# Host-side layouts, layer 0 opening on projections of raw memory, and four narrow projections per layer made wide

## The reference

```python
def hybrid_layer(x, mem, ...):
    h = rms_norm(x, norm_pre)
    proj = h @ w_in                       # 1024 x (18 blocks of 512, 8 gate columns, 5120 gates)
    y_sb = stick_breaking(sb_q, sb_k, sb_v)
    q_ml, k_ml = silu(causal_conv(ml_q, conv_q)), silu(causal_conv(ml_k, conv_k))
    h_ml = mlstm(q_ml, k_ml, ml_v, ml_i + b_igate, ml_f + b_fgate)
    y_gm = spatial_gating(gelu(gm_u), gelu(gm_v), gm_ln_g, gm_ln_b, gm_ws, gm_bs)
    y_rt = head_norm(retention(rotary(rt_q), rotary(rt_k), rt_v))
    mkv = rms_norm(mem, mem_norm) @ w_mem_kv          # 256 memory rows, 1024 -> k and v
    mem_k, mem_v = jnp.split(mkv, 2, axis=-1)
    y_xa = memory_attention(xa_q, mem_k, mem_v)
    merged = sum over 5 branches of sigmoid(gate) * (y * silu(z)) @ w_up
    return x + rms_norm(merged @ w_out, norm_post)
```

## Time and profile before

| what | us |
|---|---|
| median of 3 runs (1751.6 to 1752.3) | 1752.22 |
| span of the profiled execution | 1750.3 |
| TensorE busy in it | 1740.1 |
| VectorE busy | 1283.1 |
| ScalarE busy | 1024.5 |

### The profile page before, as it was taken

The page is one execution under the profiler, slowest core; times in us unless marked ns, Lnnn a source line. Parts: engine busy times, 40 slices in busy tenths (PEclk is TensorE's granted clock), DMA queues, the critical chain, the costliest instruction groups (busy, mean ns, idle before and its releaser), DMA issues.

```text
span 1750.3 us, 24767 instructions
## 1 busy us (share of the span) xinstructions
PE 1740.1 (99%) x9406; PEld 1512.0 (86%) x9406; DVE 1283.1 (73%) x1714; ACT 1024.5 (59%) x1417; POOL 114.3 (7%) x186
## 2 busy tenths in 40 slices
PE   9999999999999999999999999999999999999998
PEld 8988898888889888888889988888888988888887
DVE  6966676665877586757669787688778987678775
ACT  7865566454666655644555765755556656555544
POOL 5000000000000000000000000500003360000000
PEclk9999999999999999999999999999999999999999
DMA  9656654566765566565666664456665515356663
GB/s 303 193 157 178 177 169 151 175 190 186 213 181 160 166 181 175 156 181 169 191 195 197 182 192 157 144 182 193 192 186 186 171 36 181 121 169 188 188 189 109
DMA packets 204070, 306.64 MB, mean 175 GB/s; under 512 B 12362, under 2 KB 100340, under 8 KB 203824
## 3 DMA queue, kind: packets, MB, share of 16 engines
q1 hardware_dynamic: 201056, 298.91, 56.1%
q0 software_dynamic: 2896, 6.15, 1.1%
HBM read 303.97 MB, written 1.05 MB: 174 GB/s over the span
## 4 chain that ended last, share of the span: by engine, by line
PE 91%; DVE 6%; ACT 1%; issue 1%; DMA 0%; DVEq 0%; ACTq 0%
PE bank L1696 52%; PE bank L1761 22%; PE bank L1728 8%; DVE bank L1573 2%; DVE weights_lo L1056 2%; PE bank L1801 1%; PE bank L1815 1%; PE bank L2093 1%; PE bank L2111 1%; PE bank L1823 1%; PE bank L1784 1%; ACT weights_hi L583 1%; PE bank L2017 0%; PE bank L1982 0%; PE bank L2065 0%
## 5 line engine op out<-in xcount | busy, mean ns | idle before, releaser
L1056 DVE TENSOR_TENSOR weights_lo<-weights_raw,weights_hi 128x1024 fp32r<-128x1024 f32 x560 | 668.9, 1233 | 248.6 <-ACT weights_hi L583 243.7
L583 ACT ACTIVATE weights_hi<-weights_raw 128x1024 fp32r<-128x1024 f32 x560 | 574.8, 1056 | 386.0 <-DMA weights_raw<-in_w_in_dram 181.3
L1696 PE MATMUL bank<-weights_hi,h_parts 128*128 128x512 f32 x1856 | 567.6, 391 | 0.4 <-DVE h_parts L1478 0.2
L1696 PEld LDWEIGHTS bank<-weights_hi,h_parts 128*128 128x128 f32 x1856 | 348.1, 188 | 73.3 <-DVE h_parts L1478 0.6
L1696 PE MATMUL bank<-weights_lo,h_parts 128*128 128x512 f32 x928 | 348.0, 390 | 0.0
L1696 PE MATMUL bank<-weights_hi,arena_parts 128*128 128x512 f32 x928 | 270.1, 391 | 0.0
L1761 PE MATMUL bank<-h_parts,weights_hi 128*128 128x512 f32 (+1 forms) x992 | 241.0, 385 | 0.5 <-DVE arena L1110 0.4
L1696 PEld LDWEIGHTS bank<-weights_lo,h_parts 128*128 128x128 f32 x928 | 174.4, 188 | 35.3
L1696 PEld LDWEIGHTS bank<-weights_hi,arena_parts 128*128 128x128 f32 x928 | 173.6, 188 | 35.4
L1761 PEld LDWEIGHTS bank<-h_parts,weights_hi 128*128 128x128 f32 x992 | 175.3, 189 | 31.8 <-DVE arena L1110 0.9
L1696 PE MATMUL bank<-weights_lo,arena_parts 128*128 128x512 f32 x464 | 158.4, 390 | 0.0
(11 more groups left out here) (326 smaller groups left out, 1667.6 us busy)
## 6 DMA issues: line engine op xcount, KB each, us to landing
weights_raw<-in_w_in_dram SPq DMA_DIRECT2D x224, 512.0 KB, 3.7
weights_raw<-in_f_w_up_dram SPq DMA_DIRECT2D x96, 512.0 KB, 3.5
weights_raw<-in_f_w_down_dram SPq DMA_DIRECT2D x48, 512.0 KB, 3.6
weights_raw<-in_w_up_dram SPq DMA_DIRECT2D x40, 512.0 KB, 3.5
weights_raw<-in_c_w_pw_dram SPq DMA_DIRECT2D x24, 512.0 KB, 3.6
weights_raw<-in_ab_w_in_dram SPq DMA_DIRECT2D x20, 512.0 KB, 3.8
weights_raw<-in_w_mem_kv_dram SPq DMA_DIRECT2D x16, 512.0 KB, 3.6
weights_raw<-in_w_out_dram SPq DMA_DIRECT2D x16, 512.0 KB, 3.6
```

The costliest lines, as they stand in the source:

```text
L583: nc.scalar.activation(w_hi[:, q % SPLIT, 0:w], raw[:, n % RAW, 0:w], ACT.Copy).then_inc(hi_done, 1)
L1056: tt(w_lo[:, n % RAW, 0:w], raw[:, n % RAW, 0:w], w_hi[:, q % SPLIT, 0:w].bitcast(F32), ALU.subtract)\
L1696: return mm(bs[t][:, :], sp_[:, 2 * u + kk, t * P:(t + 1) * P], wp[:, kk, :], start=first and u == us[0] and kk == 0 and n == 0, stop=last ...
```

## The change

1. The host hands over the memories transposed (`memT`, `mem_2T`), all small vectors as columns (`columns`, `columns_2`) and gm_ws transposed (`gm_wsT`). The transposes on TensorE for these go, and some 50 small DMAs.
2. Layer 0 opens with mk and mv. The raw transposed memory, scaled by mem_norm's gains, is split by VectorE (L1154, L1156 of the new kernel) and projected at once; the root mean square of each memory row comes later as a factor: as a broadcast product (`mrs`, two fp32 products of 128 columns per layer) that scales mk and memT, and as ScalarE's scale on the copy of mv. The rows of the memory are still loaded, for their squares alone. x is loaded behind the first four units.
3. sb_q, ml_q, ml_k and xa_q go from `proj_F` (or its staged form) to `proj_W`. VectorE sums their banks; the convolutions read them from SBUF.

```diff
-                win(l, SBQ)
+                else:
+                    ap = kmaj("w_mem_kv", (l,))
+                    got.extend((True, ap[:, 4 * u:4 * u + 4, i * S:(i + 1) * S]) for u in range(2) for i in range(2))
+                    mem_v()
+                halved("w_in", (l,), SBQ)
...
+                if n == 4:
+                    for t, s in enumerate((x0_in, x1_in)):
+                        sp.dma_start(xs[:, t, :], A["x"][0][t * P:(t + 1) * P, :]).then_inc(s, 16)
...
+            pool.dma_start(arena[:, 6:8, :], A["mem"][0].rearrange("(t p) d -> p t d", p=P)).then_inc(mem_in, 16)
...
+            def mem_norm(src):
+
+                for t in range(NT):
+                    for n in range(2):
+                        square(src[:, t, n * 512:(n + 1) * 512], "mem", t, n)
+                for t in range(NT):
+                    act.wait_ge(vec_done, after_vec(f"mem.base{t}"))
...
+                    act.dma_start(cols[:, :], A["columns"]).then_inc(cols_in, 16)
                     log_exp_table()
+                    up_to(4)
...
+                        up_to(4 + 2 * t)
                         act.wait_ge(s, 16)
...
+                    act.wait_ge(mem_in, 16)
+                    mem_norm(rows_of(6))
+                    for t in range(NT):
+                        copy(tok(5)[:, t, :], "mv", t, ACT.Copy, f"mv{t}", scale=mem_rstd[t])
...
+                b = filled("mrs")[:, 0:S].unsqueeze(1)
                 if l == 0:
...
+                    link(tt(feat(4), feat(4), b.to_broadcast([P, 4, S]), ALU.mult), "mk")
+                else:
+                    dve.wait_ge(mem2T_in, 16)
+                link(tt(memT[:, :, :], memT[:, :, :], b.to_broadcast([P, KD, S]), ALU.mult), "memn", ("free", "mrs", 0))
...
+                    idle(6)
+                    for u in range(2):
+                        for i in range(2):
+                            proj_H("mk", i, M_HL["L0"], (u,), opening=True)
+                    proj_T("mv", src=M_HL["L0"])
...
-                proj_F("sbq", **NORMED)
...
+                proj_W("sbq", staged=True)
...
-                proj_F("mlq")
-                proj_F("mlk")
+                proj_W("mlq")
+                proj_W("mlk")
...
-                proj_F("xaq")
+                proj_W("xaq")
```

More of the change, by code:

```diff
@@ L136, in build @@
         wsT = sb("spatial_weights", [P, 4, P])
[L137 to L140, removed]
+        ident_r = sb("ident_parts", [P, P], F32R)
         cols = sb("vector_columns", [P, 104])
@@ L154, in build @@
         epsc = st[:, 10, 0:1]
+        mem_rstd = [st[:, 11, t:t + 1] for t in range(NT)]
         ps = [ctx.enter_context(nc.psum_tensor(f"bank{i}", [P, 512], F32)) for i in range(BANKS)]
@@ L811, in layer @@
                 head_norm("rt")
-                for i in range(2):
-                    copy(feat(2)[:, 2 * i:2 * i + 2, :], "xaq", i, ACT.Copy, f"xaq{i}", view=halves)
                 for t in range(NT):
@@ L1204, in layer @@
                 if l:
-                    whole_norm(rows_of(17), rows_of(17), "mem", "mem.n")
+                    for t in range(NT):
+                        base("mem", t)
                 if l == 0:
@@ L1772, in proj_H @@
                                 low_half()
+                    elif opening:
+                        for kk in range(4):
+                            if at[0] == 1 and kk == 0:
+                                pe.wait_ge(first_hi, 1)
+                            if at[0] == 1 and kk == 2:
+                                pe.wait_ge(hi_done, 1)
+                            pe.wait_ge(vec_done, VC.at(f"m_lo{4 * u + kk}"))
+                            for j in range(2):
+                                part(j, kk, 0, bs[j].rearrange("p n s -> p (n s)"), src[2][:, 4 * u + kk].rearrange("p n s -> p (n s)"))
+                        low_half()
                     else:
@@ L1839, in idle @@
             def idle(n):
-                zeros = sec(20)[:, 0:S]
+                zeros = sec(16)[:, 0:S]
                 for _ in range(n):
@@ L1873, in layer @@
                 proj_T("sbv")
-                m = rows_of(17 if l else 6)
-                pe.wait_ge(vec_done, VC.at("mem.n1"))
-                for i in range(4):
-                    turn("memT", i, m)
+                pe.wait_ge(act_done, SC.at("mem.rstd1"))
+                b = begin("mrs")
+                for t in range(NT):
+                    ins = mm(b[:, t * P:(t + 1) * P], mem_rstd[t].to_broadcast([P, P]), ident, start=True, stop=True)
+                end(ins, "mrs")
                 proj_T("sbz")
```

295 lines of the change are left out of this document (125 added, 170 removed), and 4 rows, old and new, of the table _INS.

## The result

The changed kernel takes **1778.14 us** (median of 4 runs, 1777.63 to 1778.31), the kernel before 1752.01 beside it (4 runs): a ratio of 1.0149, 95% interval 1.0134 to 1.0163. I had forecast 1753.4 in a range of 1747 to 1759, so the prediction is wrong, by 24.7 us and on the side of "slower". The profiled execution has a span of 1776.4 us against 1750.3. Further down, one execution of the kernel before and one of `c_back_fill` took some 3545 us, twice the time of all others; the medians leave them out.

What follows compares the result with a forecast made beforehand. TensorE, busy 99% of the span, was taken to bound the kernel through its own work plus its waits. From 1752.2, 7.6 us for a later opening less 6.4 saved (2.1 + 2.6 + 1.7) gave 1753.4 us, range 1747 to 1759.

Steps and rivals of the forecast that it cites:

- read as free: VectorE's four new sums of 0.70 us per wide projection hide behind the following products, costing nothing.
- Narrow to wide, 0.32 us a projection: ml_q, ml_k, xa_q in two layers save 0.32 us each, 1.9; with layer 1's sb_q, 2.1 us.
- Rival D: Projections: the number of products costs nothing, so the 2.1 us saving goes, 1755.5 us; chance 5%.
- rival C: First attention: VectorE's new sums reach TensorE, costing 2 to 3 us a layer, up to 1758; chance 8%.
- Transposes that go, -2.6: Memory's 16 transposes, 1.75 us a layer, replaced by two fp32 products, 0.44: gain 1.3 a layer, 2.6.
- I leave the wait at 0.8 and its range at 0 to 1.5: Layer 1: TensorE's 0.8 us wait for a normalised memory row stays, between 0 and 1.5 us.
- The opening: Start to sb_k: sb_k starts at 51.5 us against a mark of 43.9, so 7.6 us later.
- mv's third unit: Opening, unit 6: lo half split at 31.8 us, behind the late roots; TensorE waits 4.1 us for it.
- VectorE is 8 x 1.16 behind 30.6: Opening: VectorE splits units 6 to 13 in a row, done at 39.9 us, then makes eight lo parts.
- Before unit 4 nothing decides: Opening: mk is done at about 19 us, and TensorE waits 3 us for mv anyway.
- Rival B: Opening: clock falls in the wait before mv's third unit, 2.0 us a stretch; 1755.4, twice 1757.4; chance 20%.
- The profile shows no fall, as TensorE never rests 4 us in it: Within rival B: the before profile has no clock fall, since TensorE never rests 4 us there.

Runs made afterwards that it cites:

- c_back_fill: c_all with the logarithm steps late as in the changed kernel, and 13 products of constants put ahead of sb_y in each layer: 1756.57 us.
- c_late: Changed kernel, behind the opening: logarithms before ml_k's convolution, layer 1 memory scaling before lambda steps, last two retention-norm products behind gm_y's evacuation: 1761.39 us.
- c_all: Changed kernel with c_late's orders plus an altered opening (memory roots, rows and constants later, mv copied later, splits six ahead): 1748.14 us, ratio 0.9976.
- a_logs: Changed kernel with the first attention's four logarithm steps on VectorE moved ahead of ml_k's twelve convolution steps: 1768.62 us.
- a_memn: Changed kernel with layer 1's scaling of the transposed memory moved ahead of the four lambda steps on VectorE: 1776.08 us.
- a_memlate: Changed kernel with the DMA of the memory's rows held back until four units are split: 1779.47 us.
- c_idle: c_all with nine idle products in front instead of six: 1748.37 us.
- a_roots: Changed kernel with the memory's squares and roots moved behind the gate columns, and layer 0's mv copied unscaled and scaled there: 1775.35 us.
- a_idle: Changed kernel with 13 idle products in front instead of 6: 1781.15 us.
- a_ahead: Changed kernel with VectorE's lo splits of units 9 to 13 ahead of its wait for the transposed features: 1774.32 us.

## Why the prediction was wrong

Three steps failed, all of them waits that the prediction had put at nothing or in another place. The sums of the wide products, "read as free", cost 11.2 us (8.8 at sb_y, 2.4 at gm_y's bank); VectorE's order of splits, and the clock behind two waits, made the opening 8.4 us later than forecast; the bank that memn holds cost some 5.4. These come to 25.0 of the 24.9 us in the spans, and 9.7 of them are the slow clock (an estimate, half of the work time in the stretches: 1.7 behind each of four waits, 2.9 behind the fifth), for which the forecast had no term. The agreement is better than its parts: `c_late` gives back 18.4 us behind the opening, where the terms there come to 16.6, and the other 1.8 I can't place.

- *Narrow to wide, 0.32 us a projection.* Right. Where nothing waits, the pair ml_q and ml_k takes 22.34 on the chain of `c_all`, against 23.04: 0.35 each. Rival D falls: the number of products counts. (By the rule of columns in the Trainium skill, "TensorE: Matmul & The Clock Gate", "Back-to-back issue gap", it would have been 0.1, an estimate from the page; the trace disagrees.) The row, from the chain of `c_all` in layer 1:

```profile
535.75 22.34 PE bank L1759 x128
```

- *"They are read as free."* This step failed, and it is the largest single error. For ml_q and ml_k it cost 8.8 us: 5.4 of waits and two slow stretches (`a_logs` took 9.5 back). I had the place as rival C with 8% and priced it at 2 to 3 us a layer. What I counted was VectorE's added work, 5.6 us, against 6.9 us of slack. What I left out is that the sums are two queues' work in turn: the taps of ScalarE wait for the sums, the convolution for the taps, and weight splits lie between. I also gave layer 0 the slack of layer 1: it waited 3.25 us against 2.2. For xa_q the sums lie ahead of the evacuation of gm_y, 1.2 us a layer: I had not looked at that queue at all.
- *Transposes that go, -2.6, and "I leave the wait at 0.8 and its range at 0 to 1.5".* The saving is there, as far as the 7.2 us in all bear it out. The range of the wait was the wrong one: I followed who waits for the new product, not who waits for its bank. memn holds `mrs` until 557.1, and it cost 3.7 and a slow stretch of 1.7, 5.4 us by this trace, of which I had none. (`a_memn` gave back 5.1, part of it by a stretch that did not come; `c_late` less `a_logs` 6.3 beyond gm_y's 2.4.)
- *The opening.* mv's third unit was forecast at 31.8 and came at 32.07, unit 13 and the roots as said; since mk ended late, TensorE waited 2.6 us for it and not 4.1. Wrong was "VectorE is 8 x 1.16 behind 30.6": the program has three splits there, a wait for the transposes, and five splits behind it. In a list of instructions, where waits don't show, these are eight in a row. I had taken ScalarE's order of splits for that of both engines. That is 3.4 us of waits and 2.9 of slow clock; 1.7 more is the slow stretch behind mv's wait. With 0.3 for the unit itself these are 8.3 of the 8.4 us.
- *Before unit 4 nothing decides.* Right (`a_memlate`, `c_idle`), although mk ended at 23.8 and not at 19, after a wait of 3.7 us and at 1.2 GHz: the memory's rows, 1 MB on another queue, shared the bandwidth with the first weights (ScalarE had these at 5.7 us once the rows were held back, at 9.2 otherwise). The six idle products end at 6.2, as the rows give it (5.40 + 3 x 0.25), and not at 5.9; that decides nothing.
- *Rival B.* The mechanism was right and the chance of 20% far too low: not one or two stretches but six, five of which cost time. Its price was 2.0 us each; `c_back_fill` measured 1.6. I set it against a forecast whose own terms were waits of 3 to 4 us, and should have priced the clock beside each of them. "The profile shows no fall, as TensorE never rests 4 us in it" was also a misreading: TensorE rests for the last 6.6 us of the span of the kernel before, from 1743.66 us on, and the clock falls there:

```profile
1745.00:1746.00 1.00, 0.00 (x0) 0.00 (x0) 0.93 (x2) 0.90 (x5) 0.00 (x0) 1.00 0.00 0
...
1747.00:1748.00 1.00, 0.00 (x0) 0.00 (x0) 0.00 (x0) 0.00 (x0) 0.00 (x0) 0.50 1.00 406
```

## What to carry to other kernels

On a kernel that keeps TensorE 99% busy, price a wait like these, of 2.2 to 3.7 us, with the slow stretch that may stand behind it, and count every engine's program order through the change, also that of the steps that merely move: VectorE had time enough for its new work (1309 us busy for 1283), and moving four of its instructions gave back what the sums had cost at sb_y. When a step gets a PSUM bank of its own, ask who is given that bank next and what must be done before. And when a change loses, undo orders before undoing the idea: the same products in another order were faster than the kernel before.

## What the chip showed that I had not expected

The same wait is not followed by the same slow stretch each time. The wait for memn in layer 1 lasted 3.7 us in the changed kernel and in `a_roots`; behind it came 3.4 us at 1.2 GHz in the one and none in the other:

```profile
550.00:556.00 6.00, 2.28 (x15) 1.89 (x13) 3.79 (x6) 5.50 (x12) 0.00 (x0) 1.00 0.41 123
556.00:562.00 6.00, 6.00 (x34) 5.27 (x35) 4.37 (x8) 5.31 (x9) 0.00 (x0) 1.00 0.19 44
```

A wait of 3.1 us at sb_y in `a_memn` had none either, the one of 2.2 in the changed kernel had 3.4 us, and about the waits of 0.6 and 2.4 at sb_y of layer 0 in `a_idle` there were 10.2 at 1.2 GHz. So a kernel with such waits need not have a single time: `a_ahead` ran from 1771.4 to 1777.3, `c_all`, which hardly waits, within 1.6 us over ten runs. It need not scatter either: the changed kernel, with all of its waits, stayed within 0.7 us in four runs. What decides it stays open. The Trainium skill ("TensorE: Matmul & The Clock Gate", "What's actually happening") says of the start of a kernel that where the level changes varies from run to run; here that holds for waits in its midst too.
